# The second attention's low-part score product over 64 partitions instead of 128

## The reference

```
sc = jnp.einsum('bhqd,bhkd->bhqk', qi, k, preferred_element_type=jnp.float32)
sc = sc * scale + ci[..., None] - c[:, :, None, :]        # fox: key_pos <= tq
...
sc = jnp.where(valid, sc * scale + bias[None], NEG)        # chunk band: 8 chunks of 64 back
p = jax.nn.softmax(sc, axis=-1).astype(v.dtype)
```

## Time and profile before

| what | value |
|---|---|
| median of 3 runs | 1804.76 us |
| the profiled execution's own time | 1806.2 us |
| its span, first to last instruction | 1804.4 us |
| mean granted TensorE clock | 0.998 |
| PE busy, share of the span | 1785.7 us, 99% |
| DVE, ACT, POOL busy | 75%, 47%, 26% |
| matmuls | 8847 |
| scores of the second attention | 548.8 to 1001 us |

### The profile page before, as it was taken

How to read it: one execution, slowest core, us unless ns; L and a number is a source line. 1 busy time by engine, 2 the same in 40 slices (tenths; PEclk the granted TensorE clock), 3 DMA queues, 4 the chain that set the end, 5 groups by cost and what they waited for, 6 DMA issues and landing times.

```text
span 1804.4 us, 25144 instructions
## 1 busy us (share of the span) xinstructions
PE 1785.7 (99%) x8847; PEld 1497.4 (83%) x8847; DVE 1350.2 (75%) x2569; ACT 855.8 (47%) x1660; POOL 474.8 (26%) x434
## 2 busy tenths in 40 slices
PE   9999999999999999999999999999999999999998
PEld 7888778877888888888888878888888887888877
DVE  7698574887546877778879797697667678677777
ACT  6697133545335655555657434352223234334334
POOL 0110010013320000023323153016566645323223
PEclk9999999999999999999999999999999999999999
DMA  5101413343332222222225337434444477546243
GB/s 214 47 25 36 147 42 99 129 137 110 112 111 94 65 60 76 63 61 90 70 67 202 133 95 235 146 105 140 157 163 153 157 272 275 189 143 223 100 127 130
DMA packets 82700, 225.57 MB, mean 125 GB/s; under 512 B 8784, under 2 KB 16272, under 8 KB 79504
## 3 DMA queue, kind: packets, MB, share of 16 engines
q1 hardware_dynamic: 82160, 223.58, 37.1%
q10 hardware_dynamic: 416, 0.39, 0.1%
HBM read 161.52 MB, written 52.99 MB: 119 GB/s over the span
## 4 chain that ended last, share of the span: by engine, by line
PE 87%; DVE 6%; ACT 3%; DMA 2%; issue 2%; POOL 0%; DVEq 0%; SPq 0%; POOLq 0%; ACTq 0%
PE D L1051 53%; PE S L1051 14%; PE T L1051 6%; PE PV L1413 4%; PE T L1379 3%; PE S L1351 2%; PE S L1352 2%; PE D L1092 1%; DVE acc L1442 1%; DVE xe L2110 1%; ACT SPs L2436 1%; DVE T L2225 1%; DVE xe L2233 0%; DMA T<-fs_scratch 0%; DMA T<-f_scratch 0%
## 5 line engine op out<-in xcount | busy, mean ns | idle before, releaser
L1051 PE MATMUL D<-Hh,Wh 128*128 128x512 f32 x1052 | 280.7, 398 | 1.8 <-ACT tg L2663 1.0
L2706 ACT CAST Wh<-Wr 128x1024 fp32r<-128x1024 f32 (+2 forms) x186 | 151.4, 814 | 272.2 <-PE D L1051 207.8
L1051 PE MATMUL D<-Hh,Wl 128*128 128x512 f32 x1052 | 275.6, 393 | 0.0
L1051 PE MATMUL D<-Hl,Wh 128*128 128x512 f32 x1052 | 273.9, 392 | 0.0
L1051 PEld LDWEIGHTS D<-Hh,Wh 128*128 128x128 f32 x1052 | 192.3, 188 | 42.9 <-issue 3.4
L1051 PEld LDWEIGHTS D<-Hl,Wh 128*128 128x128 f32 x1052 | 194.5, 188 | 38.0
L1051 PEld LDWEIGHTS D<-Hh,Wl 128*128 128x128 f32 x1052 | 193.6, 188 | 37.3
L2132 DVE TENSOR_TENSOR Wl<-Wr,Wh 128x1024 fp32r<-128x1024 f32 (+2 forms) x179 | 181.4, 1013 | 41.2 <-ACT Wh L2706 40.6
L2706 ACT CAST Wh<-Sx 128x512 fp32r<-128x512 f32 (+1 forms) x120 | 70.4, 592 | 139.9 <-PE D L1051 69.2
L2132 DVE TENSOR_TENSOR Wl<-Sx,Wh 128x512 fp32r<-128x512 f32 (+1 forms) x120 | 107.9, 908 | 26.4 <-ACT Wh L2706 25.7
L2448 ACT ACTIVATE SP<-SP,sm 128x640 f32<-128x640 f32 (+7 forms) x128 | 94.5, 738 | 64.4 <-DVE sm L1653 63.8
(11 more groups left out here) (384 smaller groups left out, 3673.1 us busy)
## 6 DMA issues: line engine op xcount, KB each, us to landing
Wr<-w SPq DMA_DIRECT2D x62, 512.0 KB, 3.5
f_scratch<-xe SPq DMA_DIRECT2D x28, 768.0 KB, 5.1
Wr<-wdn SPq DMA_DIRECT2D x34, 512.0 KB, 4.4
Wr<-wo SPq DMA_DIRECT2D x32, 512.0 KB, 3.5
Wr<-wup SPq DMA_DIRECT2D x27, 512.0 KB, 3.9
T<-f_scratch SPq DMA_DIRECT2D x11, 1024.0 KB, 7.6
Hl<-f_scratch SPq DMA_DIRECT2D x10, 1024.0 KB, 6.5
K<-K SPq DMA_DIRECT2D x32, 256.0 KB, 3.4
```

Of the source, the lines that this page charges most:

```text
L1051: m = e.matmul(into, (low if n == 2 else high)(k), (operand_low if n == 1 else operand_high)(k), start=begin and (n, k) == todo[0], stop=( ...
L2706: e.copy(high, src).then_inc(*raised("act_weights", x))
```

## The change

The second score product contracts over the 64 partitions of the head alone. It so computes query high x key low, and no longer query low x key low. Nothing reads the copy of the low keys in the other partitions any more, so the transfer copies part 0 alone, and its cost in the planner falls from `load(256)` to `load(128)`. The first attention's keys (`k1`, tile Ks) are copied as before.

```diff
@@ scores() @@
-                            q = QQ[pr % 2][:, hh, qb * 128:qb * 128 + 128]
+                            q, own = QQ[pr % 2][:, hh, qb * 128:qb * 128 + 128], slice(64 * hh, 64 * hh + 64)
                             o = psum[bank[x]][:, 0:a1 - a0]
                             e.matmul(o, q, K2[pr % 2][:, hh, 0, k0 * 128 + a0:k0 * 128 + a1], start=True, stop=False)
-                            e.matmul(o, q, K2[pr % 2][:, hh, 1, k0 * 128 + a0:k0 * 128 + a1], start=False, stop=True
-                                     ).then_inc(*raised("pe_qk", x))
+                            e.matmul(o, q[own, :], K2[pr % 2][own, hh, 1, k0 * 128 + a0:k0 * 128 + a1], start=False,
+                                     stop=True).then_inc(*raised("pe_qk", x))
                             yield 2 * max(109, 12 + (a1 - a0) * 0.422)
@@ keys_across() @@
-                    e.dma_start(K[there, h, :, cs].bitcast(F32), K[here, h, :, cs].bitcast(F32)).then_inc(*landed(name, pr))
-                    yield load(256)
+                    parts = slice(0, 2 if pr == "k1" else 1)
+                    e.dma_start(K[there, h, parts, cs].bitcast(F32), K[here, h, parts, cs].bitcast(F32)).then_inc(
+                        *landed(name, pr))
+                    yield load(256 if pr == "k1" else 128)
```

## The result

The changed kernel takes 1875.47 us (median of 4 runs, 1874.22 to 1876.52) against 1804.47 us for the kernel before on the same chip. The ratio is 1.0395, with a 95% interval of 1.0383 to 1.0407: slower by 71 us. Forecast were 1875 us and a range of 1838 to 1890 us.

What follows compares the result with a forecast made beforehand. The prediction took PE, busy 99% of the span, to bound the kernel. It added 73 us for switching rows, took off 3 us given back, counted transfers, shorter matmuls and order at 0: 1804.8 + 70 = 1875 us, range 1838 to 1890.

Steps and rivals of the forecast that it cites:

- What bounds the kernel: Second attention's score stretch: PE busy 452.21 of 452.70 us, so its added work reaches the end almost one to one.
- The transfers: 32 key copies shrink from 256 to 128 KB; no PE wait in the stretch is for one, so 0.
- Fewer rows make no matmul shorter: Second score product, 192 matmuls: columns set the time, halved rows save 0; at most 13 us.
- The switch: PE going from 128 to 64 rows and back around line 1352: 192 x 0.38 = 73 us, ends 58 and 81.
- The 0.10 us by which a load starts late: Weight loads at both ends of the 16-row transposes start 0.10 us after the array would be free.
- the full matmul's open load: Load of the full matmul behind a narrow one is not hidden: 0.11 us lie open.
- the open load of the narrow matmul: Load over 64 rows lies open before its score piece's stream: 0.08 us, between 0.06 and 0.11.
- What is given back: Exposed loads, waits and idle time on PE in the score stretch partly vanish: 3 us off, bounds 0 and 6.
- The new order: A projection's four matmuls change places with two score pieces: 0, plus or minus 3 us.
- A: Rival: the switch to 64 rows costs half, 192 x 0.20 = 38 us, giving 1843 us; chance 0.10.
- C: Rival: switch free, copies land sooner, exposed loads ahead of line 1351 go, up to 6 us; 1800 us; chance 0.04.
- B: Rival: a 64-row matmul runs like a 128-row one, its load hidden; 1805 us, within 0.2%; chance 0.06.

Runs made afterwards that it cites:

- copy_order: Changed kernel (halved copies, its order) with the second score product again over 128 partitions, reading the keys' high parts: 1803.39 us, ratio 0.9993.
- order_only: Kernel before with only the planner's cost of the key copies lowered to load(128), giving the changed kernel's order: 1804.20 us, ratio 1.0002.
- third64: Changed kernel with the second score product over 64 partitions made twice in a row: 1906.21 us, ratio 1.0560.
- third128: Kernel before with its second score product over 128 partitions made twice in a row: 1834.23 us, ratio 1.0161.
- paired: Changed kernel, but where a query block has two pieces, both full products come first, then both over 64 partitions: 1858.70 us, ratio 1.0298.
- rows_only: Kernel before with only the second score product contracting over the head's 64 partitions, copies and order unchanged: 1875.38 us, ratio 1.0394.

## Why the prediction was right

**What bounds the kernel.** Right: PE's 71 us went into the end one to one, and the stages around the stretch kept their length within about 1 us.

**The transfers, priced at 0.** Right: copy_order and order_only lie within 0.1% of the kernel before.

**Fewer rows make no matmul shorter.** Right, and only now shown: third64 and third128 pay 30.7 and 30.0 us for the same columns. Half the stream would have been some 15 us less.

**The switch.** The mechanism was right in both directions and in its number, 192 (paired). The 0.10 us by which a load starts late, read off two places with 16 rows, was 0.09, and the full matmul's open load, read as 0.11, was 0.105. The term that was mis-sized is the open load of the narrow matmul, taken as 0.08 between 0.06 and 0.11: it is 0.105 us at 64 rows, and no shorter at 32. The reading of 0.06 came from small loads behind each other, and that distance isn't an open load in front of a stream.

**What is given back.** Priced at 3 us. Summed over all 192 pieces, the starts put line 1352 115 ns later behind line 1351 than before (0.306 instead of 0.191 on average), and what follows 188 ns later behind line 1352 (0.354 instead of 0.166). That makes 58.2 us. The matmuls behind the switch add 0.10 us in the 109 cases in which it is one of line 1051, 11.0 us. Where it is the next piece's line 1351 (46 cases), its load is in the 115 ns already, and the 37 others (transposes, values) had part of their loads open before and add about 2.4 us. The sum is 71.6 us, and the stretch grew by 71.1. So nothing to speak of was given back by waits. Instead not every journey pays in full. The last load is not wholly open anew in the 37 cases, and in the 16 pieces of 128 columns the distance between starts was already 0.11 us before, so the narrow load adds 0.05 us less. The price of 0.39 us on a full journey is 0.37 on average. The error in the load and the error in what is given back cancelled, and 192 x 0.38 - 3 = 70 us met 71 by that. That the forecast came within 1 us of the measured time is luck as far as these two terms go.

**The new order, 0 plus or minus 3 us.** Right: 1.0002.

**The rivals.** A (half a price) and C (a gain) fell with rows_only; all four parts of a journey that the timelines show are paid, two late starts of a load and two open loads. B fell because the loads of line 1352 no longer start with the matmul ahead. The Trainium skill ("TensorE: Matmul & The Clock Gate", section Part 3: Packing small matmuls — row/col tiling) lets a load overlap matmuls in flight only where its row group differs. That is not the case here, since the 64 rows are among the 128 of the matmul ahead, so the rule gave B no support, and no run tests it with rows that differ. Between full matmuls, which share all their rows, the loads do overlap, so the trace does not bear out the rule's "only". The rule on which the forecast's case leaned, that a change of the tiling mode drains TensorE ("TensorEngine Tiling (Array Packing)" of the Trainium skill, section Key Properties), agrees with all runs: the price is paid at each change between 128 and 64 or 32 rows, not between two matmuls over 64 (third64), and 96 rows pay next to nothing.

What stays open: whether the array pays for going from 64 rows to 32 as well, and whether narrow products on both halves of the rows, into different banks, would run side by side. No run had either. Of the kernels here none beats the kernel before, as the narrow product saves no time that could be set against its switches.

## What to carry to other kernels

On an engine that is never idle, a matmul that contracts over 64 partitions or fewer saved nothing here in a stream of full ones, and cost 0.3 to 0.4 us each time the stream goes over to it and back: let it run over all 128 rows instead, as the kernel before does, or, where products must be narrow, let them follow each other. Before such a change, look in the profile for any narrow matmul that is there already and measure from its full neighbour to its full neighbour; eight transposes of 16 rows gave this forecast. In a profile the switch shows not in PE's busy share but as idle time of PEld ahead of a load with "issue" as its releaser. By itself that sign proves nothing: the kernel before has 21 such gaps (6.9 us) with no narrow matmul beside them, and behind the shorter matmuls of the first attention only 14 of 64 narrow loads showed it. The distances between starts decide.

## What was not expected

96 rows are almost free. The ratio was 1.0011 (1.0002 to 1.0020) with 192 matmuls over 96 partitions among full ones, the loads hidden as for 128, while 64 and 32 rows both cost 70 to 71 us (1875.38 and 1875.30). Between 96 and 64 rows the price has a step, and from 64 to 32 it does not grow.
